# Modulation rows of four groups turned to columns by a product with a two-column table

## The reference

```
mod = silu(cond) @ w_mod + b_mod      # cond: c (latent) or c_ctx (context); w_mod: 1024 x 6144
shift1, scale1, gate1, shift2, scale2, gate2 = split(mod, 6)
h = rmsnorm(x, g_norm1) * (1 + scale1) + shift1
x = x + gate1 * mixer(h)              # w_in, convolution, gated linear attention, w_out
h = rmsnorm(x, g_norm2) * (1 + scale2) + shift2
x = x + gate2 * expert_choice_moe(h)  # 16 SwiGLU experts
y = rmsnorm(x, g_final)
```

## Time and profile before

| | |
|---|---|
| median of three runs | 889.68 us |
| span of the profiled execution | 889.4 us |
| TensorE busy | 867.2 us, 98% |
| TensorE weight loads | 480.7 us, 54% |
| VectorE, ScalarE, GpSimd busy | 32%, 26%, 9% |
| mean granted TensorE clock | 0.997 |

### The profile page before, as it was taken

How to read it: one execution, slowest core, us unless ns; L and a number is a source line. 1 busy time by engine, 2 the same in 40 slices (tenths; PEclk the granted TensorE clock), 3 DMA queues, 4 the chain that set the end, 5 groups by cost and what they waited for, 6 DMA issues and landing times.

```text
span 889.4 us, 14543 instructions
## 1 busy us (share of the span) xinstructions
PE 867.2 (98%) x6341; PEld 480.7 (54%) x6341; DVE 286.5 (32%) x610; ACT 229.0 (26%) x451; POOL 83.2 (9%) x83
## 2 busy tenths in 40 slices
PE   6999999999999999999999999999999999999995
PEld 5798899989998875333333333333333333333332
DVE  3576544777465574201101101101101101101123
ACT  5566634462351333101101101101101101101114
POOL 1000000000000021111011011011011011011013
PEclk9999999999999999999999999999999999999998
DMA  9864714523148358999999999999999999999973
GB/s 329 279 220 165 278 65 136 192 96 134 69 157 349 123 206 303 375 384 410 397 383 412 402 382 409 402 384 409 403 383 415 397 383 412 400 382 410 422 259 135
DMA packets 52770, 272.39 MB, mean 306 GB/s; under 512 B 6378, under 2 KB 16654, under 8 KB 40420
## 3 DMA queue, kind: packets, MB, share of 16 engines
q1 hardware_dynamic: 44908, 255.15, 73.1%
q0 software_dynamic: 6128, 10.89, 5.2%
q10 hardware_dynamic: 1672, 5.43, 1.5%
HBM read 257.95 MB, written 14.55 MB: 306 GB/s over the span
## 4 chain that ended last, share of the span: by engine, by line
PE 91%; DVE 3%; DMA 3%; ACT 1%; SPq 1%; issue 1%; POOLq 0%; POOL 0%; DVEq 0%
PE pair L2275 25%; PE pair L1892 15%; PE pair L2320 13%; PE pair L2305 13%; PE pair L2333 6%; PE pair L2131 5%; PE pair L1832 2%; PE pair L1927 2%; DMA scale_b<-in_w_mod 2%; PE pair L2234 1%; PE pair L2290 1%; DMA p1w<-in_w_out 1%; PE pair L2059 1%; PE pair L2296 1%; PE pair L2050 1%
## 5 line engine op out<-in xcount | busy, mean ns | idle before, releaser
L2275 PE MATMUL pair<-ring,xT 128*64 128x512 f32 x1024 | 223.9, 594 | 0.3 <-ACT xT L1086 0.3
L2275 PEld LDWEIGHTS pair<-ring,xT 128*64 128x64 f32 x1024 | 71.9, 137 | 142.1 <-issue 141.9
L2305 PE MATMUL pair<-ring,xT 128*32 128x512 f32 x1024 | 116.5, 595 | 0.9 <-DVE xT L1694 0.9
L2320 PE MATMUL pair<-ring,aT 128*64 128x512 f32 x512 | 116.9, 598 | 0.0
L1108 ACT ACTIVATE act_l<-pair 128x512 f32<-128x512 f32 x16 | 9.6, 597 | 290.8 <-PE pair L2275 290.8
L1703 DVE TENSOR_TENSOR act_l<-act_l,pair 128x512 f32<-128x512 f32 x16 | 11.0, 687 | 207.9 <-ACT act_l L1108 207.9
L1892 PE MATMUL pair<-hT_hi,w_hi 128*128 128x320 f32 x320 | 75.9, 319 | 0.0
L1892 PE MATMUL pair<-hT_lo,w_hi 128*128 128x320 f32 x320 | 73.1, 310 | 0.0
L1892 PE MATMUL pair<-hT_hi,w_lo 128*128 128x320 f32 x320 | 72.9, 309 | 0.0
L2320 PEld LDWEIGHTS pair<-ring,aT 128*64 128x64 f32 x512 | 34.0, 136 | 69.5 <-issue 68.2
L2305 PEld LDWEIGHTS pair<-ring,xT 128*32 128x32 f32 x1024 | 30.2, 109 | 73.1 <-issue 73.1
(11 more groups left out here) (307 smaller groups left out, 933.0 us busy)
## 6 DMA issues: line engine op xcount, KB each, us to landing
ring<-in_w_gate SPq DMA_DIRECT2D x32, 2048.0 KB, 30.3
ring<-in_w_up SPq DMA_DIRECT2D x32, 2048.0 KB, 19.4
ring<-in_w_down SPq DMA_DIRECT2D x32, 2048.0 KB, 25.1
p1w<-in_w_mod SPq DMA_DIRECT2D x8, 2048.0 KB, 8.3
p1w<-in_w_in SPq DMA_DIRECT2D x5, 2048.0 KB, 8.0
p1w<-in_w_mod SPq DMA_DIRECT2D x7, 1024.0 KB, 12.3
x_sb<-in_x_sample SPq DMA_DIRECT2D x8, 512.0 KB, 4.9
p1w<-in_w_out SPq DMA_DIRECT2D x2, 2048.0 KB, 8.0
```

The source lines that it names most:

```text
L2275: ins = mm(ps[64 * n:64 * n + 64, :], xt[:, kk, 0:CAP_L], w[:, j, n * 512:(n + 1) * 512], start=kk == 0, stop=kk == KC - 1)
L2305: ins = mm(ctx_ps[32 * g:32 * g + 32, :], xt[:, kk, CAP_L:96], w[:, j, n * 512:(n + 1) * 512], start=kk == 0, stop=kk == KC - 1)
L2320: ins = mm(y_ps[0][r:r + 64, :], aT[:, j, 64 * fh:64 * fh + 64], wd[:, j, n * 512:(n + 1) * 512], start=fh == 0 and j == 0, stop=fh == 1 a ...
```

## The change

`mod_turn` multiplies instead of transposing: the tile of `mod_rows` stays the stationary side, and the moving side is `pick`, 128 x 2, which is 1 where the row is 32g + r for the column r. The product gives the two sums over the four groups in two columns. VectorE makes `pick` once from the identity, before it waits for the parameters. Its reduction in each unit and the signal `mod_sum` are gone; the addition of the bias reads PSUM, and its signal `mod_ready` frees the pair.

```diff
+        pick = small("pick", [P, 2])
...
-            read_by[f"modT{u}"] = [(mod_sum, i + 1)]
+            read_by[f"modT{u}"] = [(mod_ready, i + 1)]
...
+            dve.wait_ge(const_ready, 2)
+            v.tensor_reduce(pick[:, :], ident[:, :].rearrange("p (g r) -> p r g", g=4)[:, 0:2, :], AX.X, ALU.add
+                            ).then_inc(pick_ready, 1)
             pp = result(dve, "prm")
             v.tensor_copy(param[:, 0:R_ALL], pp[:, 0:R_ALL]).then_inc(param_ready, 1)
...
                 n = cols.stop - cols.start
-                src = pp[:, 0:n * P].rearrange("p (j g r) -> p j r g", j=n, g=4)[:, :, 0:2, :]
-                v.tensor_reduce(mod[:, cols, :], src, AX.X, ALU.add).then_inc(mod_sum, 1)
-                dve.wait_ge(mod_sum, MOD_ORDER.index(u) + 1)
                 bias = second[:, u - 6, :] if u in (6, 7, 8, 9) else param[:, R_BMOD + cols.start:R_BMOD + cols.stop]
-                v.tensor_tensor(mod[:, cols, :], mod[:, cols, :], bias.unsqueeze(2).to_broadcast([P, n, 2]),
+                v.tensor_tensor(mod[:, cols, :], pp[:, 0:2 * n].rearrange("p (j r) -> p j r", r=2), bias.unsqueeze(2).to_broadcast([P, n, 2]),
                                 ALU.add).then_inc(mod_ready, 1)
...
                 pp = claim(pe, f"modT{u}")
+                pe.wait_ge(pick_ready, 1)
                 for j in range(mod_width(u) // P):
                     cols = slice(j, 512, 4) if u in (6, 7, 8, 9) else tile(j)
-                    ins = turn(pp[:, tile(j)], mod_rows[:, i % 2, cols], ident[:, :])
+                    ins = mm(pp[:, 2 * j:2 * j + 2], mod_rows[:, i % 2, cols], pick[:, :], start=True, stop=True)
                 end(ins, f"modT{u}")
```

More of the change, by code:

```diff
@@ L351, in build @@
         names = """job_done prm_in tail_in decay_in st_in const_ready mask_ready param_ready silu_ready o_root
-            part_ready decay_zero modrow_ready mod_sum mod_ready scale_ready ss_ready root_ready
+            part_ready decay_zero modrow_ready pick_ready mod_ready scale_ready ss_ready root_ready
             xr_ready hT_low hT_high raw_even raw_odd hT_hi_ready hT_ready whi_ready wlo_ready yThi_ready yTlo_ready alow_ready qk_first qk_second abs_ready min_ready softplus_ready cum_ready
@@ L362, in build @@
         (job_done, prm_in, tail_in, decay_in, st_in, const_ready, mask_ready, param_ready, silu_ready, o_root,
-         part_ready, decay_zero, modrow_ready, mod_sum, mod_ready, scale_ready, ss_ready, root_ready,
+         part_ready, decay_zero, modrow_ready, pick_ready, mod_ready, scale_ready, ss_ready, root_ready,
          xr_ready, hT_low, hT_high, raw_even, raw_odd, hT_hi_ready, hT_ready, whi_ready, wlo_ready, yThi_ready, yTlo_ready, alow_ready, qk_first, qk_second, abs_ready, min_ready, softplus_ready, cum_ready,
```

## The result

The changed kernel takes 902.04 us in the median (898.57 to 902.58, four runs) against 889.74 us; the ratio is 1.012 with a 95% interval of 1.0108 to 1.0132. The forecast was slower, 893.9 us with a range to 896.3; the direction was right and the size less than half of what came: some 12 us instead of 4. The profiled execution has a span of 900.5 us, 11.1 more than before, and its own time is 902.58 us. The times of the changed kernel lie 2.1 to 2.3 us above their spans, those of the kernel before 1.7 to 1.8, wherever an execution lists both; the prediction took 0.3, from a median and a span that weren't of one execution.

What follows compares the result with a forecast made beforehand. TensorE was taken as the bound: 48 product tiles at 0.22 instead of 0.11 us add 5.3 us, less 1.1 swallowed by idle time, +4.2 on 889.7, so 893.9 us; range 892.3 to 896.3.

Steps and rivals of the forecast that it cites:

- a plain tile: Modulation units on TensorE: a product tile costs 0.22 us against 0.11 for a transpose; 48 tiles add 5.3 us.
- VectorE's sum: Removing 16 reductions of 178 ns on VectorE: worth 0 beyond the 0.2 us counted at 48.19.
- the chain over VectorE: Unit 3b to row 6's tokens: the longer product (+0.22 us) and the missing reduction with its gap (0.21) cancel.
- the strided loads: Units 6 to 9, 32 loads at a stride of four elements: taken as 0 extra, with 2.3 us as upper end.
- the rival: Units 6 to 9: strided product loads slower by 0.07 us on 32 loads, +2.3 us, 896.2 us; chance 0.12.
- The swallowed time: TensorE's idle time at four places (24.54, 28.98, 48.19, 229.79 us) takes up 1.1 us of the added work.
- the three places in the quarters: Idle time of TensorE at 24.54, 28.98 and 48.19 us, taking up 0.3, 0.2 and 0.2 us.
- 28.98: 2b's transposes wait for the pair 0b's reduction reads; 0b's 0.22 us fits into the idle time: 0.2 us swallowed.
- 48.19: Row 6's first products wait for tokens from unit 3b; the idle 0.19 takes 3b's 0.22: 0.2 us swallowed.
- 24.54: TensorE waits for the weights of 2b; 0.3 of the 0.44 us that 0a and 2a add is swallowed.
- 229.79: attention(2) waits for yT behind a DMA, ScalarE and VectorE; 0.4 of unit 8's 0.44 us is swallowed.

Runs made afterwards that it cites:

- one pass: Changed kernel with neighbouring columns in every load and rows and table in float32r, one load and one matmul a product: 890.24 us, ratio 0.9995.
- plain_units_only: Changed kernel with the product only in the quarters and units 4, 5, 10, 11; units 6 to 9 transposed and summed as before: 893.61 us, ratio 1.0035.
- the larger samples: The kernel before, unchanged, run on the same chip as the follow-up experiments: medians of 890.6 to 891.0 us.

## Why the prediction was wrong

**What held.** TensorE sets the pace, 96 loads and 96 matmuls came, and a plain tile costs 0.22 us against 0.11: a quarter's four loads 0.44 us with the piece behind (0.34 + 0.10), unit 5's eight 0.79 and 0.10 behind. By the runs with one pass and with the plain units it is the second load that costs. The page of the Trainium skill cited in the prediction gives 107 ns for a load of 128 columns, worked out from its rule; the plain loads agree in their distance of 0.11 us, though the trace lists 192 ns for one. VectorE's sum was worth 0, as said. In the quarters the chain over VectorE kept its length: from the end of the projection ahead of unit 3b to hT_lo it is 2.72 us before (44.52 to 47.24) and 2.64 after (44.71 to 47.35), so the longer product and the missing reduction nearly cancel.

**The step that failed: the strided loads.** The prediction said "That row is nearest to the strided case, so I take 0, and keep 2.3 us as the end." The row was L1818's, four strided loads of transposes, 0.11 us apart. Measured, a strided load of a product is 1.73 / 8 = 0.22 us from the next, 3.5 us for the 32 of them. The row was of another kind of instruction: transposes and products load differently (141 and 188 ns when plain), and the strided transposes already showed the sign, 213 against 141. Nor does the length of a load give its distance: the strided transposes, 213 ns, make a unit 0.47 us instead of 0.44, 0.12 us a tile. Adding the difference of 0.07 us to each load, as the rival did, was also too little. And the rule of the Trainium skill for a load ("TensorE: Matmul & The Clock Gate", LDWEIGHTS), its columns over 1.2 GHz, has no term for the stride; here the measurement decides against it: twice the distance at a stride of four elements.

**What the prediction left out: the clock.** No rival named it. All rows of this stretch before the change had full clock, also behind rows of transposes, and I took the clock as given. The sum had no term for it, and no reason for leaving it out. Two falls cost 2.86 + 1.53 = 4.4 us in the profiled execution, and with 128 moving columns neither appears in the traces. When two-column matmuls bring a fall isn't settled. Eight on plain loads did it in no trace. Sixteen on plain loads did it in the one trace that had them; of the other three executions two had none by their mean clocks, and one is undecided. Eight on strided loads behind unit 8 did it in three traces of five, behind unit 7 in one of five, and behind unit 9, with no two-column matmuls directly ahead of it, in one of three. With the plain ones of unit 4 ahead of them, those of unit 9 did it in all three traces, with one pass and with two.

**The swallowed time.** 1.1 us was forecast. In plain_units_only 0.5 of 3.5 us is missing, and that kernel has the three places in the quarters and not the last. At 28.98 and 48.19 the idle time is gone, as forecast; at 24.54 the profiled execution of the changed kernel never waited (it began 2b at 23.91, the weights had landed), so that place depends on the execution; at 229.79 the wait is gone as well, since TensorE comes there later by the 1.26 us more of unit 8 (1.73 - 0.47) and by the fall.

The account of the changed kernel over the kernel before then is: 48 tiles at 0.11 us more, 5.3; the stride, 3.5; less 0.9 swallowed (0.5 and the 0.4 at 229.79); 7.9 together. The execution of 898.57 us, which by its mean clock of 0.996 had no fall, lies 8.8 above the 889.74 beside it and 7.6 to 8.0 above the medians of the larger samples. The 0.4 us outside the span is in no term, so the account holds to about half a us. The falls, up to 4.4, make the rest. What stays open is when exactly the clock falls: the traces of the one program have two and three falls, and by its mean clock one execution had none.

## What to carry to other kernels

A product is not a transpose with the sum thrown in: in this kernel a float32 product loaded its stationary tile twice, and with two moving columns the loads were the whole price but for the clock. Read the price of a load from a row of the same kind of instruction and the same stride, or make it contiguous where another engine writes the tile anyway. And before work with very few moving columns is put on a busy TensorE, count the clock as something that it can cost: what comes behind pays.

## What the runs showed of the hardware that I had not expected

- A weight load of 128 float32 columns for a product took 192 ns and stood 0.11 us from the next; at a stride of four elements 330 ns and 0.22 us, in two passes and in one. For transposes the stride made it 213 instead of 141 ns, and 0.12 instead of 0.11 us a tile.
- The granted clock fell from 2.4 to 1.2 GHz while TensorE was busy, toward the end of 16 two-column matmuls, for 6.8 us; the same loads with 128 columns left it at 2.4 GHz in the trace, and so did the transposes in that place before the change.
- The same program took 898.6 to 903.9 us at mean clocks from 0.996 down to 0.990, where all executions of the kernel before lie between 889.4 and 891.8.
